# First norm of a hybrid decoder layer: two groups of tiles with a root each, all squares on ScalarE, the root's table loaded at the start

## The chip, the cores and the metric

The kernel runs on one core of one Trainium2 chip. The metric is the device time of one execution in microseconds (us). Engines: PE is TensorE (matmul), PEld its weight loads, DVE VectorE, ACT ScalarE, POOL GpSimd, SP SyncE, which here issues the DMAs.

## The reference

One layer on 16 learned meta tokens and 512 real tokens of width 2048. The change lies in the first `rms_norm`; everything else follows it.

```python
def rms_norm(x, g):
    xf = x.astype(jnp.float32)
    y = xf * lax.rsqrt(jnp.mean(xf * xf, axis=-1, keepdims=True) + RMS_EPS)
    return (y * g.astype(jnp.float32)).astype(x.dtype)

h = jnp.concatenate([meta, x], axis=1)
hn = rms_norm(h, ln_mix_g[l])
proj = hn @ w_in[l]                      # 2048 -> 5632 columns
...                                      # attention and HGRN2 on proj
h = h + jnp.concatenate([att, rec], axis=-1) @ w_out[l]
h = h[:, N_META:]
h = h + peer_ffn(rms_norm(h, ln_ffn_g[l]), ...)
```

## The kernel before, in words

The program is a row of blocks: first norm (tag `mixnorm`), projection, attention, recurrence, output product, second norm (tag `ffnnorm`), routing, gate tables, experts. In a block each engine has its own instruction list, the lists meet only through semaphores, and a barrier stands between blocks. Within an engine instructions start in the order written, so a wait holds all that is queued behind it.

`norm_rows` writes a norm block. The first norm has five sources in this order: the meta rows (16 partitions), then four tiles of 128 tokens (`x_rows`, tile numbers 0 to 3). SyncE issues, in order, two early constants, the meta rows, the four tiles (1 MB each), the first four pieces of `w_in` and the other constants; `loaded[i]` counts the landing of source i. `stat` holds small rows per tile: 0 the sum of squares, 1 the mean plus epsilon, 2 its square root, 3 the inverse root.

- ACT (L151 to L176) squares and sums the meta rows and tiles 0, 1 and 3 (L163), waiting for each landing and for its own previous sum; then takes one square root for all five sources (L167), splits the high parts of two pieces of `w_in` (L311), and copies 16 column blocks out of PSUM with the gain (`hn_high`, L172).
- DVE (L187 to L223) squares tile 2 (`by_dve`, L197), waits for all sums, makes the mean (L203), waits for the root, corrects it in five small chained operations (`inverse_root`, L102 to L106), scales the four tiles (L208) and the meta rows (L211), and then makes the low parts of the 16 column blocks (`hn_low`, L214) and of the meta rows (L219, L223).
- PE (L226 to L252) waits for each scaled tile and turns its first six column blocks with matmuls against the identity (L232, six PSUM banks), then the meta rows (L244), then the other ten column blocks, each as soon as DVE has emptied the bank of six blocks before.
- POOL narrows a mask that comes with the last constant (L2300) and subtracts the two low parts of `w_in` (L319).

The second norm uses the same function with `sums` given, hence without squares and with no meta rows.

Of the kernel before, what the change touches and what calls it, by code (L numbers as in the profile page):

```python
# [24 lines left out]
ALU = mybir.AluOpType  # L25
ACT = mybir.ActivationFunctionType
AX = mybir.AxisListType
F32 = mybir.dt.float32
# [4 lines left out]
P = 128  # L33
D = 2048
DC = D // P
T = 512
TB = T // P
# [8 lines left out]
EPS = 1e-6  # L46
# [13 lines left out]
class Count:  # L60
# [10 lines left out]
    def link(self, ins):  # L71

        self.up(ins)
        self.wait()
# [25 lines left out]
def inverse_root(dve, link, out, square, root, spare):  # L100

    link(dve.reciprocal(out, root))  # L102
    link(dve.tensor_tensor(spare, out, out, ALU.mult))
    link(dve.tensor_tensor(spare, spare, square, ALU.mult))
    link(dve.tensor_scalar(spare, spare, -0.5, 1.5, ALU.mult, ALU.add))
    link(dve.tensor_tensor(out, out, spare, ALU.mult))  # L106
# [5 lines left out]
def norm_rows(nc, tag, tiles, scaled_tiles, meta, gain, parts, columns, ident, place, kb, stream,  # L112
              loads, consts=None, sums=None, pool_first=None, pool_last=None, split_here=True):

    n = len(tiles) + (meta is not None)
    hi, lo = parts
    used = []
    with ExitStack() as ctx:
        def sem(name):
            used.append(ctx.enter_context(nc.semaphore(f"{tag}_{name}")))
            return used[-1]

        loaded = [sem(f"loaded{i}") for i in range(n)] if sums is None else []
        summed, summed_too, meaned, rooted = sem("summed"), sem("summed_too"), sem("meaned"), sem("rooted")  # L130
        scaled, turned, high, low = sem("scaled"), sem("turned"), sem("high"), sem("low")
        meta_turned, meta_whole_ready, meta_high = (sem("meta_turned"), sem("meta_whole_ready"),
                                                    sem("meta_high"))
        chain = sem("chain")
        stat = place(f"{tag}_stat", [P, 4, 8], F32, kb)
        squares = [place(f"{tag}_squares{i}", [P, D], F32, kb + 1 + 8 * i) for i in range(2)] \
            if sums is None else []
        meta_whole = place(f"{tag}_meta_whole", [P, DC, M], F32, kb + 17) if meta is not None else None
        banks = [ctx.enter_context(nc.psum_tensor(f"{tag}_bank{b}", [P, TB, P], F32)) for b in range(NORM_BANKS)]
        meta_bank = ctx.enter_context(nc.psum_tensor(f"{tag}_meta_bank", [P, DC, M], F32))  # L140
        block = ctx.enter_context(nc.Block())
        by_dve = 2

        def sources():

            return ([(meta, M, TB)] if meta is not None else []) + [(rows, P, tb) for tb, rows in enumerate(tiles)]

        @block.sync
        def _(sp):
            loads(sp, loaded)  # L150

        @block.scalar
        def _(act):
            act.wait_ge(chain, 1)
            if sums is None:
                count = 0
                for i, (rows, m, at) in enumerate(sources()):
                    if at == by_dve:
                        continue
                    act.wait_ge(loaded[i], 16)  # L160
                    if count:
                        act.wait_ge(summed, count)
                    act.activation(squares[0][0:m, :], rows, ACT.Square,  # L163
                                   accum_out=stat[0:m, 0, at:at + 1]).then_inc(summed, 1)
                    count += 1
            act.wait_ge(meaned, 1)
            act.activation(stat[:, 2, 0:n], stat[:, 1, 0:n], ACT.Sqrt).then_inc(rooted, 1)  # L167
            if split_here:
                stream.split_first_high(act)
            for c in range(DC):  # L170
                act.wait_ge(turned, c + 1)
                act.activation(columns(hi, c), banks[c % NORM_BANKS][:, :, :], ACT.Copy,  # L172
                               scale=gain[:, c:c + 1]).then_inc(high, 1)
            if meta is not None:
                act.wait_ge(meta_whole_ready, 1)
                act.copy(hi[:, :, 0:M], meta_whole[:, :, :]).then_inc(meta_high, 1)  # L176

        @block.gpsimd
        def _(pool):
            if pool_first:  # L180
                pool_first(pool)
            if split_here:
                stream.split_first_low(pool)
            if pool_last:
                pool_last(pool, scaled)

        @block.vector  # L187
        def _(dve):
            link = Count(dve, chain).link
            link(dve.memset(stat[:, 0, :], 1.0))  # L190
            if consts:
                dve.wait_ge(*consts)
            if sums is None:
                for i, (rows, m, at) in enumerate(sources()):
                    if at == by_dve:
                        dve.wait_ge(loaded[i], 16)
                        dve.scalar_tensor_tensor(squares[1][:, :], rows, 1.0, rows, ALU.mult, ALU.mult,  # L197
                                                 accum_out=stat[:, 0, at:at + 1]).then_inc(summed_too, 1)
                dve.wait_ge(summed, n - 1)
                dve.wait_ge(summed_too, 1)  # L200
            else:
                link(dve.tensor_reduce(stat[:, 0, 0:TB], sums[:, :, :], AX.X, ALU.add))
            dve.tensor_scalar(stat[:, 1, 0:n], stat[:, 0, 0:n], 1.0 / D, EPS,  # L203
                              ALU.mult, ALU.add).then_inc(meaned, 1)
            dve.wait_ge(rooted, 1)
            inverse_root(dve, link, stat[:, 3, 0:n], stat[:, 1, 0:n], stat[:, 2, 0:n], stat[:, 0, 0:n])
            for tb in range(TB):
                dve.tensor_scalar(scaled_tiles[tb], tiles[tb], stat[:, 3, tb:tb + 1], None, ALU.mult)\  # L208
                    .then_inc(scaled, 1)
            if meta is not None:  # L210
                dve.tensor_scalar(meta, meta, stat[0:M, 3, TB:TB + 1], None, ALU.mult).then_inc(scaled, 1)  # L211
            for c in range(DC):
                dve.wait_ge(high, c + 1)
                dve.scalar_tensor_tensor(columns(lo, c), banks[c % NORM_BANKS][:, :, :], gain[:, c:c + 1],  # L214
                                         columns(hi, c).bitcast(F32), ALU.mult, ALU.subtract)\
                    .then_inc(low, 1)
            if meta is not None:
                dve.wait_ge(meta_turned, 1)
                dve.tensor_tensor(meta_whole[:, :, :], meta_bank[:, :, :],  # L219
                                  gain[:, :].unsqueeze(2).to_broadcast([P, DC, M]), ALU.mult)\  # L220
                    .then_inc(meta_whole_ready, 1)
                dve.wait_ge(meta_high, 1)
                dve.tensor_tensor(hi[:, :, M:2 * M], meta_whole[:, :, :], hi[:, :, 0:M].bitcast(F32),  # L223
                                  ALU.subtract)

        @block.tensor  # L226
        def _(pe):
            if consts:
                pe.wait_ge(*consts)

            def turn(tb, c):
                return pe.transpose(banks[c % NORM_BANKS][:, tb, :], scaled_tiles[tb][:, c * P:(c + 1) * P],  # L232
                                    ident[:, :])

            for tb in range(TB):
                pe.wait_ge(scaled, tb + 1)
                for c in range(NORM_BANKS):
                    last = turn(tb, c)
                    if tb == TB - 1:
                        last.then_inc(turned, 1)  # L240
            if meta is not None:
                pe.wait_ge(scaled, n)
                for c in range(DC):
                    last = pe.transpose(meta_bank[:, c, :], meta[:, c * P:(c + 1) * P], ident[0:M, 0:M])  # L244
                last.then_inc(meta_turned, 1)
            for c in range(NORM_BANKS, DC):
                pe.wait_ge(low, c - NORM_BANKS + 1)
                for tb in range(TB):
                    last = turn(tb, c)
                last.then_inc(turned, 1)  # L250
    return used
# [2166 lines left out]
```

## Time and profile before

| | us |
|---|---|
| median of 3 runs | 3525.15 (3524.41 to 3530.05) |
| the profiled execution, its own time | 3515.08 |
| its span, first to last instruction | 3513.3 |
| PE busy | 3337.3 (95%) |
| DVE / ACT / POOL busy | 2222.2 / 1116.2 / 1186.5 |
| first norm, from the start to the first matmul of the projection | 38.08 |

A row of the timeline gives start, duration, engine, line, operation, out<-in, count, and in brackets how long the engine sat idle before it and what released it. A row with a count of several is merged; its duration then goes from the first start to the last end.

### The profile page before, as it was taken

The numbers are of one execution on the slowest core, as the hardware profiler recorded it, in microseconds if no ns is written. First come the engines' busy times: TensorE is split into PE (matmuls) and PEld (weight loads), VectorE is DVE, ScalarE is ACT, GpSimd is POOL, SyncE is SP. The second block draws the span as 40 slices with busy tenths as digits, with TensorE's granted clock in tenths as the row PEclk, the third lists the DMA queues.
The fourth block names the chain that finished last, engine by engine and source line by source line (L and its number), as shares of the span: only waits on it lengthen the run. The fifth ranks groups of instructions, "written<-read, shape, count | busy, mean of one in ns | idle before, by whom it ended". The sixth has DMA issues, their size and how long they took to land.

```text
span 3513.3 us, 51557 instructions
## 1 busy us (share of the span) xinstructions
PE 3337.3 (95%) x16860; PEld 2931.6 (83%) x16860; DVE 2222.2 (63%) x3869; ACT 1116.2 (32%) x1725; POOL 1186.5 (34%) x878
## 2 busy tenths in 40 slices
PE   7999999779989976799999999999999999999999
PEld 5778877667877866789989989989989989989998
DVE  2003413893038898677777777777777777777776
ACT  3222223443222279232232232332332322322322
POOL 2344441364435610323223233233233233333332
PEclk9999999999999999899999999999999999999999
DMA  4233320003322234878878788888878878878776
GB/s 142 78 90 96 96 84 16 25 1 118 99 101 85 84 126 203 291 261 277 262 261 278 258 263 278 259 261 273 266 261 274 264 260 271 268 259 275 265 260 235
DMA packets 294650, 686.94 MB, mean 196 GB/s; under 512 B 139040, under 2 KB 139296, under 8 KB 292000
## 3 DMA queue, kind: packets, MB, share of 16 engines
q1 hardware_dynamic: 220848, 417.52, 36.5%
q0 software_dynamic: 73728, 268.47, 22.7%
q8 instruction: 43, 0.70, 0.1%
q14 instruction: 31, 0.25, 0.0%
HBM read 655.48 MB, written 30.41 MB: 195 GB/s over the span
## 4 chain that ended last, share of the span: by engine, by line
PE 59%; ACT 2%; issue 1%; DMA 1%; DVE 1%; ACTq 0%; SPq 0%; POOL 0%; DVEq 0%; POOLq 0%
PE exp_a L2018 10%; PE exp_a L2020 10%; PE exp_a L2019 10%; PE exp_o L2039 10%; PE exp_o L2041 10%; PE exp_o L2037 10%; ACT table_gaps L1808 1%; ACT table_stage L1824 1%; DMA exp_rows<-in_u_rows,exp_now 0%; PE table_b L1768 0%; DMA gate_table<-table_stage 0%; DVE exp_rows L2123 0%; ACTq L1808 0%; DMA exp_act<-gate_table 0%; ACTq L1824 0%
## 5 line engine op out<-in xcount | busy, mean ns | idle before, releaser
L2020 PE MATMUL exp_a<-x_high,exp_ul 128*128 128x384 f32 x1984 | 663.1, 334 | 0.0
L2018 PE MATMUL exp_a<-x_high,exp_uh 128*128 128x384 f32 x1984 | 663.0, 334 | 0.0
L2019 PE MATMUL exp_a<-x_low,exp_uh 128*128 128x384 f32 x1984 | 662.9, 334 | 0.0
L2037 PE MATMUL exp_o<-exp_vh,exp_ah 128*128 128x512 f32 x1536 | 599.3, 390 | 27.4 <-DVE exp_al L2183 16.1
L2041 PE MATMUL exp_o<-exp_vh,exp_al 128*128 128x512 f32 x1536 | 599.4, 390 | 0.0
L2039 PE MATMUL exp_o<-exp_vl,exp_ah 128*128 128x512 f32 x1536 | 599.3, 390 | 0.0
L1999 POOL DMA_INDIRECT exp_rows<-in_v_rows,exp_now x256 | 330.4, 1290 | 706.9 <-DVE h L2130 655.4
L1999 POOL DMA_INDIRECT exp_rows<-in_u_rows,exp_now x256 | 299.9, 1171 | 704.4 <-DVE exp_rows L2123 658.9
L2069 ACT CAST exp_vh<-exp_raw 128x1024 fp32r<-128x1024 f32 x252 | 256.0, 1051 | 515.9 <-PE exp_o L2041 488.0
L2109 DVE TENSOR_TENSOR exp_vl<-exp_raw,exp_vh 128x1024 fp32r<-128x1024 f32 x256 | 304.4, 1220 | 155.0 <-ACT exp_vh L2069 146.0
L2018 PEld LDWEIGHTS exp_a<-x_high,exp_uh 128*128 128x128 f32 x1984 | 372.4, 188 | 1.2
L2019 PEld LDWEIGHTS exp_a<-x_low,exp_uh 128*128 128x128 f32 x1984 | 372.4, 188 | 1.2
L2020 PEld LDWEIGHTS exp_a<-x_high,exp_ul 128*128 128x128 f32 x1984 | 372.4, 188 | 0.0
L2080 ACT ACTIVATE exp_act<-exp_a 128x384 f32<-128x384 f32 x124 | 61.1, 492 | 950.0 <-PE exp_a L2020 807.6
L2037 PEld LDWEIGHTS exp_o<-exp_vh,exp_ah 128*128 128x128 f32 x1536 | 289.3, 188 | 87.3 <-issue 16.3
L2041 PEld LDWEIGHTS exp_o<-exp_vh,exp_al 128*128 128x128 f32 x1536 | 289.1, 188 | 60.2
L2039 PEld LDWEIGHTS exp_o<-exp_vl,exp_ah 128*128 128x128 f32 x1536 | 289.4, 188 | 59.5
L319 POOL TENSOR_TENSOR w_in_lo<-w_in_raw,w_in_hi 128x1024 fp32r<-128x1024 f32 x88 | 212.5, 2416 | 320.2 <-ACT w_in_hi L305 320.2
L2109 DVE TENSOR_TENSOR exp_ul<-exp_raw,exp_uh 128x1024 fp32r<-128x1024 f32 x248 | 300.2, 1221 | 31.1 <-ACT exp_uh L2069 31.1
L2130 DVE SCALAR_TENSOR_TENSOR h<-exp_rows,exp_weights,h 128x1024 f32<-128x1024 f32 x256 | 316.6, 1277 | 0.2 <-DMA exp_rows<-in_v_rows,exp_now 0.2
L2123 DVE SCALAR_TENSOR_TENSOR exp_rows<-exp_rows,sparse_x 128x1024 f32<-128x1024 f32 x256 | 302.7, 1217 | 10.6 <-DMA exp_rows<-in_u_rows,exp_now 10.5
L2150 DVE TENSOR_TENSOR exp_act<-exp_act,exp_gates 128x384 f32<-128x384 f32 x124 | 69.7, 562 | 356.7 <-ACT exp_act L2080 214.1
(302 smaller groups left out, 5263.3 us busy)
## 6 DMA issues: line engine op xcount, KB each, us to landing
exp_raw<-in_v SPq DMA_DIRECT2D x256, 512.0 KB
exp_raw<-in_u SPq DMA_DIRECT2D x248, 512.0 KB
w_in_raw<-in_w_in SPq DMA_DIRECT2D x88, 512.0 KB, 3.6
gate_table<-table_stage SPq DMA_DIRECT2D x5, 4096.0 KB, 11.5
exp_gates<-gate_table SPq DMA_DIRECT2D x126, 160.0 KB, 2.6
w_out_raw<-in_w_out SPq DMA_DIRECT2D x32, 512.0 KB, 3.7
w_q_raw<-in_w_q SPq DMA_DIRECT2D x32, 512.0 KB, 3.9
x_rows<-in_x SPq DMA_DIRECT2D x4, 1024.0 KB, 8.0
```

The lines of the kernel that those rows point to most:

```text
L319: eng.tensor_tensor(self.lo[:, g % 2], self.raw[:, g % RAW], self.hi[:, g % 2].bitcast(F32), ALU.subtract).then_inc(self.low, 1)
L1999: pool.indirect_dma_start(rows[slot][:, :], None, sparse["u" if kind == "dot" else "v"], bass.IndirectOffsetOnAxis(ap=now[:, turn, place_n ...
L2018: pe.matmul(bank, uh[:, b, c, :], xh[:, 0:DENSE_TB, c, :], start=(c == 0), stop=False)
L2019: pe.matmul(bank, uh[:, b, c, :], xl[:, 0:DENSE_TB, c, :], start=False, stop=False)
L2020: last = pe.matmul(bank, ul[:, b, c, :], xh[:, 0:DENSE_TB, c, :], start=False, stop=(c == DC - 1))
L2037: pe.matmul(bank[:, :], ah[:, key, tokens], vh[:, dc % 2, key, :], start=(key == 0), stop=False)
L2039: pe.matmul(bank[:, :], ah[:, key, tokens], vl[:, dc % 2, key, :], start=False, stop=False)
L2041: last = pe.matmul(bank[:, :], al[:, key, tokens], vh[:, dc % 2, key, :], start=False, stop=(key == KEYS_OF_MACRO - 1))
L2069: act.copy(part(uh if split[0] == "u" else vh, *split, half), raw[:, c % RAW_SLOTS, :])\
L2109: dve.tensor_tensor(part(ul if kind == "u" else vl, kind, which, half), raw[:, slot, :], part(uh if kind == "u" else vh, kind, which, half ...
L2123: done = dve.scalar_tensor_tensor(rows[slot][:, :], rows[slot][:, :], 1.0, sparse["x"][:, half, :], ALU.mult, ALU.mult, accum_out=dots[:, ...
L2130: done = dve.scalar_tensor_tensor(sums, rows[slot][:, :], weights[:, pl(pick(m, kind, t), 1)], sums, ALU.mult, ALU.add)
```

## The change

The first norm's five sources form two groups: tiles 0 and 1, and then tiles 2, 3 and the meta rows. Each group gets its own mean, root, inverse root and scaling. ACT takes all five sums of squares; the DVE square of tile 2 is gone. Before the first square ACT runs a square root over the eight freshly set ones of `stat` and writes a row that is overwritten later, so that the table that the root needs is the first one loaded. The root of the first group stands on ACT between the wait for tile 2's landing and tile 2's square. The second norm has one group, as before. The semaphore `summed_too` is replaced by `opened`, and one scratch tile of squares is gone.

```diff
-        by_dve = 2
+        groups = [slice(0, n)] if sums is not None else [slice(0, TB // 2), slice(TB // 2, n)]
...
         def _(act):
+            def root(g):
+                act.wait_ge(meaned, g + 1)
+                act.activation(stat[:, 2, groups[g]], stat[:, 1, groups[g]], ACT.Sqrt).then_inc(rooted, 1)
+
             act.wait_ge(chain, 1)
             if sums is None:
-                count = 0
+                act.activation(stat[:, 2, :], stat[:, 0, :], ACT.Sqrt).then_inc(opened, 1)
                 for i, (rows, m, at) in enumerate(sources()):
-                    if at == by_dve:
-                        continue
                     act.wait_ge(loaded[i], 16)
-                    if count:
-                        act.wait_ge(summed, count)
+                    if i == 0:
+                        act.wait_ge(opened, 1)
+                    else:
+                        act.wait_ge(summed, i)
+                    if at == groups[0].stop:
+                        root(0)
                     act.activation(squares[0][0:m, :], rows, ACT.Square,
                                    accum_out=stat[0:m, 0, at:at + 1]).then_inc(summed, 1)
-                    count += 1
-            act.wait_ge(meaned, 1)
-            act.activation(stat[:, 2, 0:n], stat[:, 1, 0:n], ACT.Sqrt).then_inc(rooted, 1)
+            root(len(groups) - 1)
...
             link(dve.memset(stat[:, 0, :], 1.0))
...
-            if sums is None:
-                for i, (rows, m, at) in enumerate(sources()):
-                    if at == by_dve:
-                        dve.wait_ge(loaded[i], 16)
-                        dve.scalar_tensor_tensor(squares[1][:, :], rows, 1.0, rows, ALU.mult, ALU.mult,
-                                                 accum_out=stat[:, 0, at:at + 1]).then_inc(summed_too, 1)
-                dve.wait_ge(summed, n - 1)
-                dve.wait_ge(summed_too, 1)
-            else:
+            if sums is not None:
                 link(dve.tensor_reduce(stat[:, 0, 0:TB], sums[:, :, :], AX.X, ALU.add))
-            dve.tensor_scalar(stat[:, 1, 0:n], stat[:, 0, 0:n], 1.0 / D, EPS,
-                              ALU.mult, ALU.add).then_inc(meaned, 1)
-            dve.wait_ge(rooted, 1)
-            inverse_root(dve, link, stat[:, 3, 0:n], stat[:, 1, 0:n], stat[:, 2, 0:n], stat[:, 0, 0:n])
-            for tb in range(TB):
-                dve.tensor_scalar(scaled_tiles[tb], tiles[tb], stat[:, 3, tb:tb + 1], None, ALU.mult)\
-                    .then_inc(scaled, 1)
+            for g, group in enumerate(groups):
+                if sums is None:
+                    dve.wait_ge(summed, n if group.stop == n else group.stop + 1)
+                dve.tensor_scalar(stat[:, 1, group], stat[:, 0, group], 1.0 / D, EPS,
+                                  ALU.mult, ALU.add).then_inc(meaned, 1)
+                dve.wait_ge(rooted, g + 1)
+                inverse_root(dve, link, *(stat[:, row, group] for row in (3, 1, 2, 0)))
+                for tb in range(group.start, min(group.stop, TB)):
+                    dve.tensor_scalar(scaled_tiles[tb], tiles[tb], stat[:, 3, tb:tb + 1], None, ALU.mult)\
+                        .then_inc(scaled, 1)
```

On ACT, from the start of the first norm to the split of `w_in`, the program before has these rows (`mixnorm_loaded0` is the landing of the meta rows, `loaded1` to `loaded4` those of tiles 0 to 3):

```order
-L163 ACT_TABLE_LOAD [waits mixnorm_loaded0]
-L163 ACTIVATE mixnorm_squares_115,mixnorm_stat<-meta_rows 16x2048 [waits mixnorm_chain]
-L163 ACTIVATE mixnorm_squares_115,mixnorm_stat<-x_rows 128x2048 [waits mixnorm_summed,mixnorm_loaded1]
-L163 ACTIVATE mixnorm_squares_115,mixnorm_stat<-x_rows 128x2048 [waits mixnorm_summed,mixnorm_loaded2]
-L163 ACTIVATE mixnorm_squares_115,mixnorm_stat<-x_rows 128x2048 [waits mixnorm_summed,mixnorm_loaded4]
-L167 ACT_TABLE_LOAD
-L167 ACTIVATE mixnorm_stat<-mixnorm_stat 128x5 [waits mixnorm_meaned]
-L311 CAST w_in_hi<-w_in_raw 128x1024 [waits w_in_loaded0]
```

In the changed program the same stretch of ACT reads:

```order
+L159 ACT_TABLE_LOAD
+L159 ACTIVATE mixnorm_stat<-mixnorm_stat 128x8 [waits mixnorm_chain]
+L168 ACTIVATE mixnorm_squares,mixnorm_stat<-meta_rows 16x2048 [waits mixnorm_opened,mixnorm_loaded0]
+L168 ACTIVATE mixnorm_squares,mixnorm_stat<-x_rows 128x2048 [waits mixnorm_summed,mixnorm_loaded1]
+L168 ACTIVATE mixnorm_squares,mixnorm_stat<-x_rows 128x2048 [waits mixnorm_summed,mixnorm_loaded2]
+L155 ACTIVATE mixnorm_stat<-mixnorm_stat 128x2 [waits mixnorm_meaned,mixnorm_summed,mixnorm_loaded3]
+L168 ACTIVATE mixnorm_squares,mixnorm_stat<-x_rows 128x2048
+L168 ACTIVATE mixnorm_squares,mixnorm_stat<-x_rows 128x2048 [waits mixnorm_summed,mixnorm_loaded4]
+L155 ACTIVATE mixnorm_stat<-mixnorm_stat 128x3 [waits mixnorm_meaned]
+L309 CAST w_in_hi<-w_in_raw 128x1024 [waits w_in_loaded0]
```

One table load is left, ahead of every landing; tile 2's square has come to ACT, and the first group's root stands ahead of it.

On DVE, the first norm before, up to the scaled meta rows:

```order
-L190 MEMSET mixnorm_stat 128x8
-L197 SCALAR_TENSOR_TENSOR mixnorm_squares_116,mixnorm_stat<-x_rows 128x2048
-L203 TENSOR_SCALAR mixnorm_stat<-mixnorm_stat 128x5
-L102 RECIPROCAL mixnorm_stat<-mixnorm_stat 128x5
-L103 TENSOR_TENSOR mixnorm_stat<-mixnorm_stat 128x5
-L104 TENSOR_TENSOR mixnorm_stat<-mixnorm_stat 128x5
-L105 TENSOR_SCALAR mixnorm_stat<-mixnorm_stat 128x5
-L106 TENSOR_TENSOR mixnorm_stat<-mixnorm_stat 128x5
-L208 TENSOR_SCALAR x_rows<-x_rows,mixnorm_stat 128x2048 x4
-L211 TENSOR_SCALAR meta_rows<-meta_rows,mixnorm_stat 16x2048
```

And in the changed program, from the end of the first group's inverse root on (the first group's mean and other chained operations, of 128x2, stand ahead of it in the same order as the second's):

```order
+L106 TENSOR_TENSOR mixnorm_stat<-mixnorm_stat 128x2
+L206 TENSOR_SCALAR x_rows<-x_rows,mixnorm_stat 128x2048 x2
+L201 TENSOR_SCALAR mixnorm_stat<-mixnorm_stat 128x3
+L102 RECIPROCAL mixnorm_stat<-mixnorm_stat 128x3
+L103 TENSOR_TENSOR mixnorm_stat<-mixnorm_stat 128x3
+L104 TENSOR_TENSOR mixnorm_stat<-mixnorm_stat 128x3
+L105 TENSOR_SCALAR mixnorm_stat<-mixnorm_stat 128x3
+L106 TENSOR_TENSOR mixnorm_stat<-mixnorm_stat 128x3
+L206 TENSOR_SCALAR x_rows<-x_rows,mixnorm_stat 128x2048 x2
+L209 TENSOR_SCALAR meta_rows<-meta_rows,mixnorm_stat 16x2048
```

Two of the four scalings now stand ahead of the last mean, and six small operations are added. The lists of PE, POOL and SP hold the same instructions in the same order as before.

## Rows read from the trace of the kernel before

**Rows 1.** The page: busy time and the span in 40 slices of 88 us.

```profile
PE 3337.3 (95%) x16860; PEld 2931.6 (83%) x16860; DVE 2222.2 (63%) x3869; ACT 1116.2 (32%) x1725; POOL 1186.5 (34%) x878
...
PE   7999999779989976799999999999999999999999
```

**Rows 2.** Busy time by stretch: start:end, length, each engine, granted clock, DMA share, GB/s.

```profile
37.00:43.00 6.00, 4.92 (x12) 3.89 (x13) 0.52 (x2) 0.01 (x1) 0.00 (x0) 0.50 0.47 128
44.00:50.00 6.00, 6.00 (x28) 4.59 (x27) 0.00 (x0) 1.05 (x1) 1.54 (x1) 1.00 0.00 1
50.00:550.00 500.00, 500.00 (x2162) 391.90 (x2160) 86.19 (x108) 116.61 (x134) 201.48 (x84) 1.00 0.30 86
550.00:1450.00 900.00, 756.80 (x4119) 641.24 (x4118) 597.97 (x1863) 386.89 (x819) 332.18 (x230) 0.94 0.28 97
1450.00:3513.30 2063.30, 2056.16 (x10463) 1878.98 (x10461) 1517.08 (x1866) 589.22 (x742) 645.51 (x557) 1.00 0.80 265
```

**Rows 3.** Timeline, ACT and DVE up to the root.

```profile
4.54 1.28 ACT L163 ACT_TABLE_LOAD   x1 [4.54 <-DMA meta_rows<-in_meta]
5.83 1.91 ACT L163 ACTIVATE mixnorm_squares<-meta_rows 16x2048 f32<-16x2048 f32 x1
7.92 1.91 ACT L163 ACTIVATE mixnorm_squares<-x_rows 128x2048 f32<-128x2048 f32 x1
10.02 1.91 ACT L163 ACTIVATE mixnorm_squares<-x_rows 128x2048 f32<-128x2048 f32 x1
12.19 2.29 DVE L197 SCALAR_TENSOR_TENSOR mixnorm_squares<-x_rows 128x2048 f32<-128x2048 f32 x1 [11.29 <-DMA x_rows<-in_x]
14.56 1.91 ACT L163 ACTIVATE mixnorm_squares<-x_rows 128x2048 f32<-128x2048 f32 x1 [2.54 <-DMA x_rows<-in_x]
16.38 0.19 ACT L163 ACTIVATION_READ_ACCUMULATOR mixnorm_squares<-x_rows 128x1 f32 x1
16.58 1.28 ACT L167 ACT_TABLE_LOAD   x1
16.60 0.17 DVE L203 TENSOR_SCALAR mixnorm_stat<-mixnorm_stat 128x5 f32<-128x5 f32 x1 [2.11 <-ACT mixnorm_squares L163]
17.88 0.21 ACT L167 ACTIVATE mixnorm_stat<-mixnorm_stat 128x5 f32<-128x5 f32 x1
17.99 1.98 ACT L311 CAST w_in_hi<-w_in_raw 128x1024 fp32r<-128x1024 f32 x2
```

**Rows 4.** Timeline, from the root to the last low part.

```profile
18.11 0.19 DVE L102 RECIPROCAL mixnorm_stat<-mixnorm_stat 128x5 f32<-128x5 f32 x1 [1.35 <-ACT mixnorm_stat L167]
19.14 4.88 DVE L208 TENSOR_SCALAR x_rows<-x_rows,mixnorm_stat 128x2048 f32<-128x2048 f32 x4
20.58 5.35 PE L232 MATMUL mixnorm_bank<-c_ident,x_rows 128*128 128x128 f32 x24 [20.58 <-DVE x_rows L208]
23.93 1.27 DVE L211 TENSOR_SCALAR meta_rows<-meta_rows,mixnorm_stat 16x2048 f32<-16x2048 f32 x1
24.90 9.37 ACT L172 ACTIVATE hn_high<-mixnorm_bank,c_ln_mix 128x512 fp32r<-128x512 f32 x16 [4.94 <-PE mixnorm_bank L232]
25.62 10.62 DVE L214 SCALAR_TENSOR_TENSOR hn_low<-mixnorm_bank,c_ln_mix,hn_high 128x512 fp32r<-128x512 f32 x16 [0.42 <-ACT hn_high L172]
```

**Rows 5.** Timeline, the weight loads of the turning matmuls.

```profile
20.55 4.98 PEld L232 LDWEIGHTS mixnorm_bank<-c_ident,x_rows 128*128 128x128 f32 x24 [20.55 <-issue]
27.16 1.73 PEld L232 LDWEIGHTS mixnorm_bank<-c_ident,x_rows 128*128 128x128 f32 x16
29.06 0.42 PEld L232 LDWEIGHTS mixnorm_bank<-c_ident,x_rows 128*128 128x128 f32 x4 [0.17 <-DVE hn_low L214]
```

**Rows 6.** Timeline, POOL in the first norm and the block's end.

```profile
26.82 0.93 POOL L2300 CAST c_level_mask<-level_mask_wide 128x896 uint8<-128x896 f32 x1 [26.35 <-DMA level_mask_wide<-in_level_mask]
27.80 4.70 POOL L319 TENSOR_TENSOR w_in_lo<-w_in_raw,w_in_hi 128x1024 fp32r<-128x1024 f32 x2
37.05 0.42 DVE L223 TENSOR_TENSOR hn_high<-mixnorm_meta_whole,hn_high 128x256 fp32r<-128x256 f32 x1 [0.47 <-ACT hn_high L176]
38.08 0.76 PE L364 MATMUL proj_bank<-w_in_hi,hn_high 128*128 128x512 f32 x1 [5.06 <-DVEq L517]
```

**Rows 7.** Timeline, matmuls of the projection: two starts early, two later.

```profile
39.06 0.63 PE L366 MATMUL proj_bank<-w_in_lo,hn_high 128*128 128x512 f32 x1
39.49 0.63 PE L364 MATMUL proj_bank<-w_in_hi,hn_high 128*128 128x512 f32 x1
...
44.10 0.39 PE L365 MATMUL proj_bank<-w_in_hi,hn_low 128*128 128x512 f32 x1
44.33 0.40 PE L366 MATMUL proj_bank<-w_in_lo,hn_high 128*128 128x512 f32 x1
```

More of the change, by code:

```diff
@@ L129, in norm_rows @@
         loaded = [sem(f"loaded{i}") for i in range(n)] if sums is None else []
-        summed, summed_too, meaned, rooted = sem("summed"), sem("summed_too"), sem("meaned"), sem("rooted")
+        summed, opened, meaned, rooted = sem("summed"), sem("opened"), sem("meaned"), sem("rooted")
         scaled, turned, high, low = sem("scaled"), sem("turned"), sem("high"), sem("low")
@@ L135, in norm_rows @@
         stat = place(f"{tag}_stat", [P, 4, 8], F32, kb)
-        squares = [place(f"{tag}_squares{i}", [P, D], F32, kb + 1 + 8 * i) for i in range(2)] \
-            if sums is None else []
+        squares = [place(f"{tag}_squares", [P, D], F32, kb + 1)] if sums is None else []
         meta_whole = place(f"{tag}_meta_whole", [P, DC, M], F32, kb + 17) if meta is not None else None
```

## The prediction

> **What bounds the kernel now.** I read the page first. PE is busy for 95% of the span, and only a few of its forty slices fall below nine tenths [rows 1]. The table of stretches says where: from 50 to 550 us PE is busy for all of the 500 us, and from 1450 us to the end for 2056 of 2063 us; between, it is busy for 757 of 900 us [rows 2]. So behind the first norm PE is nearly always at work. The weight loads from memory follow PE's pace there, because each buffer is refilled only when its use is over. A time by which the projection starts earlier should therefore reach the end of the span unchanged. The first norm itself is the one part that the change touches: PE's first matmul of the projection starts at 38.08 us [rows 6].
>
> Next I read the timeline of those 38 us and followed the wait that ends last. Tile 3 lands at 14.56 us, when ACT starts its square [rows 3]; tile 2 landed at 12.19 us, when DVE started. ACT's sum is out at 16.57 us (16.38 + 0.19). DVE makes the mean (16.60 + 0.17 = 16.77), but the root starts only at 17.88, since ACT loads a table from 16.58 for 1.28 us [rows 3]. DVE's chain runs from 18.11, the four scalings start at 19.14, the meta rows' at 23.93 [rows 4]. The last tile is scaled shortly before, PE turns it, ACT makes its first high part at 24.90 and DVE the first low part at 25.62. From there DVE goes through 16 low parts in 10.62 us, 0.66 each, and bounds the rest; its last operation ends at 37.47, and PE starts 0.61 later [rows 4, 6]. Thus the path is: landing of tile 3, square, mean, table and root, chain, four scalings, turn, 16 low parts, meta rows.
>
> **The change, part by part.**
>
> *The table load.* Before, two loads; after, one, ahead of all landings, as the order shows. The first one ran from 4.54 to 5.82 while tiles were still on their way [rows 3]. Having it earlier gains nothing, because the square of tile 3 still waits for 14.56. The second lay on the path. Now the root can start when the mean is out, 16.77 plus the 0.03 us that a hand-over takes (17.88 + 0.21 = 18.09 against 18.11, and 16.57 against 16.60) [rows 3, 4], thus at 16.80 in place of 17.88: **gain 1.08**. The dummy root at the start costs some 0.21 us [rows 3] between 1 and 4.5 us, where ACT waits for the meta rows: 0 on the path. The load's cover is the 4.54 us before the meta rows land; without it, it would cost at most its 1.28 at the start, and even then ACT would be back on the landings by tile 3.
>
> On the price of a load, the row shows 1.28 us, and 1.30 us from its start at 16.58 to the root's start at 17.88 [rows 3]. The Trainium skill (ScalarE: Activation LUTs, section "What ACT_TABLE_LOAD costs") states about 1.28 us for the load and about 1.38 us more for a drain, some 2.66 us for each switch. This trace agrees with the load and shows no drain beside it. By the page's price, as an estimate, the gain of this part would be some 2.4 in place of 1.08.
>
> *The square of tile 2.* On DVE it took 2.29 us plus its read-out; ACT's start one after another every 2.10 us (7.92, 10.02) [rows 3]. ACT now has root, square 2 and square 3 behind the landing at 12.19. The root takes 0.11 us of the queue (17.88 to 17.99, where the next instruction starts) [rows 3]. Square 2 starts at 12.30, square 3 could start at 14.40, and tile 3 lands at 14.56. **Cost 0**, with 0.16 us of cover. Were tile 2 to land later or tile 3 earlier, each tenth beyond that would be lost; if they landed together the loss would be some 2.2. I take 0, with 0.3 as the upper end, from landings that differ by a few tenths. The mean of the first group needs the sums of the meta rows, tile 0 and tile 1. ACT will start the meta rows at about 4.54 and not 5.83, so tile 1's square starts no later than 10.02, its sum is out by 12.02 and the mean by 12.22: the wait ahead of the first root ends with tile 2's landing, or 0.03 later. What is queued behind that wait is square 2 alone.
>
> The same page (section "Rules for kernel authors") says that multiplications belong on VectorE, not on ScalarE. The trace does not bear this out for this f32 square: 2.10 us from start to start on ACT against 2.29 on DVE. What hangs on it is only whether square 3 is late, and by the rows it is not.
>
> *The first group.* Its root ends about 12.5. DVE's chain from the reciprocal to the first scaling takes 1.03 us (18.11 to 19.14), and scalings start every 1.20 us ((23.93 − 19.14)/4) [rows 4]. So tiles 0 and 1 are scaled from about 13.5 to 16.0. DVE must be free for the second mean at 16.60; 0.6 us of cover. The scalings run beside DMA traffic and beside ACT, as they did before. So the six added small operations cost 0, and **two scalings leave the path: gain 2 × 1.20 = 2.40**. If the cover failed, DVE would be late by what is over, at most a few tenths.
>
> *The second group.* Mean at 16.60, root 16.80 to 17.01, chain from 17.03, tile 2 scaled from 18.06, tile 3 from 19.26, meta rows from 20.46. Before it was 23.93: 3.47 sooner. The high part of `w_in` (1.98 us on ACT) starts at 16.9 and ends at 18.9, long before ACT's first high part at about 21.4. It needs its two pieces on the chip; they were there at 17.99, and if the first came at just that time ACT would still end near 20.
>
> *Turning.* Twenty-four weight loads took 4.98 us, 0.21 each, at first; sixteen took 1.73, 0.108 each, from 27.16 on [rows 5]. PE thus ran at half pace at first, and had little slack against DVE's 1.20 us per tile (24 matmuls in 5.35). Now it turns tiles 0 and 1 early and comes to tile 3 without a backlog: between 0 and 0.2 gained, I take 0. If PE stayed at the slow pace through the whole of the norm, four matmuls would take 0.86 us against DVE's 0.66. Six full banks stand ahead; over ten blocks PE falls 2.0 us behind and has about 1.0 of lead, so 1.0 is the upper end of the cost. I take 0, since PE is at work without a long pause from 19.4 on, longer than before.
>
> *The end of the block.* POOL is fixed by a landing at 26.35, which the change doesn't move, and ends at 32.50 (27.80 + 4.70) [rows 6]. DVE now ends at 34.00. **POOL is late next**, with 1.5 us of cover. It limits any gain to about 5.0.
>
> The sum: 1.08 + 2.40 = 3.48, with bounds of 2.2 (0.3 and 1.0 lost) to 3.7 (0.2 won). Against the profiled execution this is a span of 3513.3 − 3.5 = 3509.8 and a time of 3515.08 − 3.5 = 3511.6. That execution lies 10 us below the median of the runs shown, and 9.3 below the lowest of them. Against the median: **3525.15 − 3.5 = 3521.6**, or 0.10% faster. A change within 0.2% (7 us) is about what a measurement of this kernel can't tell from none.
>
> **The rivals.**
>
> *(a) As summed*, 3521.6: 0.60.
>
> *(b) PE's clock doesn't fall ahead of the projection.* The granted clock was 0.50 from 37 to 43 us and 1.00 from 44 on [rows 2], after PE had sat idle for 5.06 us [rows 6]; these are the levels of 1.2 and 2.4 GHz. Matmuls started every 0.43 us and later every 0.23 [rows 7]. From 38.08 to about 43.5 that is 12.7 matmuls of 0.20 more, 2.5 us. The change leaves the idle stretch as long as it was, so it should fall again; but it may not, or may last for another length. If not: 3519.1. Chance 0.12.
>
> *(c) A table switch costs more than its row shows.* In this kernel ACT would have stood still beyond the 1.28 us before; the rows leave 0.02 us for that (17.88 − 16.58 − 1.28). A further 1.4 us would give 3520.2. The page named above has this rule. Chance 0.03.
>
> *(d) The gain does not arrive.* The barrier behind the norm waits for POOL. If the mask landed at 30.9 and not at 26.35, POOL would end at 37.0 and nothing would be won: 3525. Against it: the same DMAs are issued in the same order, and their landing waited for nothing on ACT or DVE. Chance 0.05.
>
> *(e) The clock in the middle, the slower side.* Between 550 and 1450 us the mean granted clock is 0.94 [rows 2]: some 108 us at the lower level (0.06 × 2 × 900), worth up to 54 us. Where PE pauses there, and when the clock follows, may change when everything starts 3.5 us sooner. Break-even is 7 us more at the lower level; 20 us more would cost 10 and give 3531.6. For it: executions of the same program differ by 5.6 us here, and by 15 with the profiled one. Against it: it isn't bound to the change and has no sign. Slower side 0.07, and the faster side, down to some 3512, 0.13, for the profiled execution shows that such times occur.
>
> **How the numbers follow.** The time is that of (a). The range takes in (a) to (d), 3519 to 3525, and the nearer part of both sides of (e): 3513.5 to 3528.5, leaving out less than 0.2. Faster by over 0.2% needs 7 us: most of the fast side of (e) and a tail of (a) and (b), 0.14. Slower by over 0.2%: most of the slow side of (e), 0.05. The rest, 0.81, is within 0.2%.
>
> **What would show it.** In the changed kernel's profile: one table load before 4.5 us, none near 16.6; square of tile 2 at 12.3 and of tile 3 at 14.56, still released by the DMA; two scalings between 13.5 and 16.0; root at 16.8; meta rows scaled from 20.5; first low part at 22.1; DVE's end at 34.0 and the projection's first matmul at 34.6. Wrong would be: tile 3's square released by ACT's own sum, the second mean released by DVE's own scaling, a POOL row released at the barrier, or a projection start at 34.6 with a span that isn't 3.5 shorter; then the difference lies in the granted clock between 550 and 1450 us.

## The result, and the profile after

The changed kernel takes 3533.43 us (median of 20 runs, 3522.13 to 3545.20); the kernel before, beside it, 3523.87 us (20 runs, 3511.97 to 3537.23). The ratio is 1.0030 with a 95% interval of 1.0019 to 1.0042: it is **slower by some 10 us** (7 to 15 by the interval), where 3.5 us less was forecast, and 3533.43 lies above the forecast range of 3513.5 to 3528.5. The profiled execution took 3527.13 us, with a span of 3525.3, against 3515.08 and 3513.3 before.

The norm itself did nearly what was forecast. Timeline of the changed kernel, the rows that answer to [rows 3, 4, 6]:

```profile
0.75 1.28 ACT L159 ACT_TABLE_LOAD   x1 [0.75 <-PEq L2409]
12.42 1.89 ACT L168 ACTIVATE mixnorm_squares<-x_rows 128x2048 f32<-128x2048 f32 x1
13.53 2.48 DVE L206 TENSOR_SCALAR x_rows<-x_rows,mixnorm_stat 128x2048 f32<-128x2048 f32 x2
14.83 1.91 ACT L168 ACTIVATE mixnorm_squares<-x_rows 128x2048 f32<-128x2048 f32 x1 [0.42 <-DMA x_rows<-in_x]
17.07 0.21 ACT L155 ACTIVATE mixnorm_stat<-mixnorm_stat 128x3 f32<-128x3 f32 x1 [0.23 <-DVE mixnorm_stat L201]
20.72 1.27 DVE L209 TENSOR_SCALAR meta_rows<-meta_rows,mixnorm_stat 16x2048 f32<-16x2048 f32 x1
22.17 11.39 DVE L212 SCALAR_TENSOR_TENSOR hn_low<-mixnorm_bank,c_ln_mix,hn_high 128x512 fp32r<-128x512 f32 x16 [0.18 <-ACT hn_high L175]
27.09 0.69 ACT L175 ACTIVATE hn_high<-mixnorm_bank,c_ln_mix 128x512 fp32r<-128x512 f32 x1 [0.17 <-PE mixnorm_bank L230]
35.39 0.47 PE L362 MATMUL proj_bank<-w_in_hi,hn_high 128*128 128x512 f32 x1 [4.26 <-DVEq L515]
```

The one table load stands at the start, two scalings run from 13.53 on, the root follows the mean at once, and the meta rows are scaled 3.21 us sooner (23.93 − 20.72). The projection starts at 35.39, 2.69 sooner. The forecast gain was 3.48. Of the missing 0.79 us, 0.27 is the landing of tile 3 (14.83 against 14.56), and 0.77 the 16 low parts, which took 11.39 and not 10.62: the high part at 27.09 waits for PE, one of five such waits, since PE was turning at the slower pace there (these high parts lie 0.85 us apart, four matmuls of 0.21). Against this, 0.24 was won between the meta rows' scaling and the first low part (1.45 us in place of 1.69).

The loss lies far behind, in the routing, which the change does not touch. Busy time by stretch, each from the first PE instruction of attention, routing, gate tables and experts to the next stage's (columns as in [rows 2]); the kernel before:

```profile
572.80:660.90 88.10, 71.00 (x427) 55.79 (x427) 62.58 (x138) 50.49 (x127) 3.40 (x6) 0.95 0.04 13
1013.60:1257.70 244.10, 229.13 (x1089) 194.38 (x1089) 185.72 (x902) 61.86 (x77) 129.11 (x54) 0.98 0.25 78
1257.70:1460.40 202.70, 140.74 (x924) 124.10 (x925) 177.08 (x502) 149.16 (x354) 25.75 (x23) 0.90 0.57 221
1460.40:3513.30 2052.90, 2045.76 (x10417) 1870.35 (x10415) 1506.67 (x1851) 586.41 (x739) 639.94 (x554) 1.00 0.80 265
```

and the changed kernel:

```profile
569.20:663.40 94.20, 78.95 (x426) 61.87 (x426) 62.79 (x138) 50.46 (x127) 3.38 (x6) 0.84 0.04 12
1016.00:1268.90 252.90, 228.41 (x1089) 193.90 (x1089) 198.00 (x902) 61.86 (x77) 129.13 (x54) 0.97 0.25 75
1268.90:1472.50 203.60, 141.92 (x925) 124.47 (x926) 177.93 (x503) 149.12 (x354) 27.05 (x23) 0.90 0.57 222
1472.50:3525.30 2052.80, 2045.70 (x10417) 1870.30 (x10415) 1505.87 (x1850) 586.56 (x739) 639.89 (x553) 1.00 0.80 265
```

Read the third busy column, DVE, in the second row of each: the same 902 instructions are busy for 198.00 us in place of 185.72, and the stretch is 8.8 us longer. The experts take the same to 0.1 us. Attention is 6.1 us longer, at a granted clock of 0.84 against 0.95; that part turned out to belong to the execution, not to the kernel (below). The two profiled spans differ by 12.0 us, and the stages add up to it: 2.7 and 0.9 less up to attention, 6.1 more in attention, 0.1 less up to the routing, 8.8 more in the routing, 0.9 more in the gate tables and 0.1 less in the experts.

Where on DVE? The same four operations, one behind the other, in the routing, kernel before:

```profile
1115.17 0.23 DVE L1676 SCALAR_TENSOR_TENSOR route_pos_f<-route_quarterf 128x64 f32<-128x64 f32 x1
1115.43 0.23 DVE L1678 SCALAR_TENSOR_TENSOR route_pos_f<-route_pos_f,route_quarterf 128x64 f32<-128x64 f32 x1
1115.69 0.23 DVE L1680 TENSOR_TENSOR route_pos_f<-route_pos_f,route_quarterf 128x64 f32<-128x64 f32 x1
1116.06 2.35 DVE L1643 TENSOR_REDUCE picks<-route_hot 128x1024 f32 x2
```

changed kernel (its lines are two lower):

```profile
1114.89 0.22 DVE L1674 SCALAR_TENSOR_TENSOR route_pos_f<-route_quarterf 128x64 f32<-128x64 f32 x1
1115.15 2.43 DVE L1676 SCALAR_TENSOR_TENSOR route_pos_f<-route_pos_f,route_quarterf 128x64 f32<-128x64 f32 x1
1117.61 0.23 DVE L1678 TENSOR_TENSOR route_pos_f<-route_pos_f,route_quarterf 128x64 f32<-128x64 f32 x1
1117.98 2.35 DVE L1641 TENSOR_REDUCE picks<-route_hot 128x1024 f32 x2
```

An operation of 0.23 us stands there with 2.43: the next one came 2.2 us late, and no wait is given for it. More such places follow in later passes, at L1667, L1678 and L1683. Grouped by line over the routing, the changed kernel shows the eight calls of L1676 with a mean of 500 ns and those of L1678 with 757:

```profile
L1678 DVE TENSOR_TENSOR route_pos_f<-route_pos_f,route_quarterf 128x64 f32<-128x64 f32 x8 | 6.1, 757 | 0.3
L1676 DVE SCALAR_TENSOR_TENSOR route_pos_f<-route_pos_f,route_quarterf 128x64 f32<-128x64 f32 x8 | 4.0, 500 | 0.3
```

where the kernel before has 225 for both:

```profile
L1678 DVE SCALAR_TENSOR_TENSOR route_pos_f<-route_pos_f,route_quarterf 128x64 f32<-128x64 f32 x8 | 1.8, 225 | 0.3
L1680 DVE TENSOR_TENSOR route_pos_f<-route_pos_f,route_quarterf 128x64 f32<-128x64 f32 x8 | 1.8, 225 | 0.3
```

The kernel before isn't free of such places. Two of them:

```profile
1063.81 2.41 DVE L1675 CAST route_quarterf<-route_pos 128x256 f32<-128x256 uint32 x1
1230.90 2.33 DVE L1654 CAST route_idx_f<-route_idx 128x128 f32<-128x128 uint32 x1 [0.24 <-DVE route_idx L1631]
```

I call a stall here a DVE row that lasts over 0.4 us longer than the median row of the same operation, shape and tiles. The routing of the kernel before then has 5 stalls, with 8.9 us in all; that of the changed kernel has 12, with 21.6 us, and these 12.7 us more are about what DVE's busy time has more (12.3). The second half of the routing is a loop of three passes of 288 DVE instructions. The kernel before stalls twice ahead of the loop, twice in its last pass and once behind it; the changed kernel stalls in every pass.

How it reaches PE is in the changed kernel's timeline, POOL and PE:

```profile
1177.18 4.75 POOL L1478 TENSOR_TENSOR route_hot<-route_hot,route_idx_f 128x1024 f32<-128x1024 f32 x2 [5.04 <-DVE route_hot L1683]
1181.88 4.71 POOL L317 TENSOR_TENSOR w_q_lo<-w_q_raw,w_q_hi 128x1024 fp32r<-128x1024 f32 x2
...
1184.29 0.50 PE L362 MATMUL route_q<-x_high,w_q_hi 128*128 128x512 f32 x1 [3.51 <-POOL w_q_lo L317]
```

POOL waits for DVE's late `route_hot`, the low part of the weights is queued behind it, and PE waits for that. Ahead of the same `route_hot` POOL sat idle for 2.70 us before and 5.04 now. Over the whole routing PE idles 15.0 us before (244.1 − 229.13) and 24.5 now (252.9 − 228.41): of DVE's 12.3 us more, 9.5 arrive at PE.

### The profile page after: what moved, and what is told of

It reads as the page before. It is cut to its first block, busy times and chain, and to the rows that moved or that the text cites. A ratio compares the mean times of both kernels' runs of the same rounds, so it can differ in the third digit from the quotient of the medians.

```text
span 3525.3 us, 51564 instructions
## 1 busy us (share of the span) xinstructions
PE 3346.7 (95%) x16860; PEld 2939.8 (83%) x16860; DVE 2233.9 (63%) x3873; ACT 1117.9 (32%) x1728; POOL 1188.5 (34%) x878
## 4 chain that ended last, share of the span: by engine, by line
PE 59%; ACT 2%; issue 1%; DMA 1%; DVE 0%; ACTq 0%; SPq 0%; POOL 0%; DVEq 0%; POOLq 0%
PE exp_a L2018 10%; PE exp_a L2016 10%; PE exp_a L2017 10%; PE exp_o L2037 10%; PE exp_o L2035 10%; PE exp_o L2039 10%; ACT table_gaps L1806 2%; ACT table_stage L1822 1%; DMA exp_rows<-in_u_rows,exp_now 0%; DMA gate_table<-table_stage 0%; PE table_b L1766 0%; DVE exp_rows L2121 0%; ACTq L1806 0%; ACTq L1822 0%; SPq L1950 0%
```

## The experiments

Two theories. **P, place:** the change lengthens DVE's instruction list by three (six small operations more; the square, its read-out and one separate wait less), so everything later on DVE, the routing too, lies at other places in the list and stalls at other instructions. **S, shift:** the earlier start itself moves the pauses of PE against the chip's decisions on its clock, and the loss is the clock's. All ratios are against the kernel before on the same chip.

**b_dve3** puts three one-element memsets into the kernel before, while DVE idles:

```diff
             link(dve.memset(stat[:, 0, :], 1.0))
+            if sums is None:
+                for k in range(3):
+                    dve.memset(pads[:, k:k + 1], 0.0)
```

> The kernel before with three one-element memsets added on VectorE, before its wait for the first tile, where it idles until 12.2 us: its instruction list is then as long as the changed kernel's, its timing in the norm is unchanged. Theory P (place in the instruction list: what comes later on VectorE is fetched at other places, and stalls there): slower than the kernel before by 5 to 13 us. Rival S (the earlier start itself, through PE's clock): same as before, within 3 us.

Measured: 3540.83 us against 3526.55, ratio 1.0039 (1.0019 to 1.0059). The memsets end by 1.1 us of an idle time that lasts to 12.18, and the projection starts at 38.1 as before. The routing's stretch, where the same 902 instructions show 201.98 us:

```profile
1026.40:1284.80 258.40, 233.99 (x1089) 197.93 (x1089) 201.98 (x902) 61.86 (x77) 128.97 (x54) 0.94 0.24 74
```

Three instructions that cost nothing where they stand make the kernel 14 us slower by the medians (7 to 21 by the interval). S falls as the main cause: nothing started earlier.

**b_act4** lengthens ScalarE's list instead, **b_dve3_act4** both:

```diff
             act.wait_ge(chain, 1)
             if sums is None:
+                for k in range(5):
+                    act.activation(pads[:, 256 + k:257 + k], stat[:, 0, 5 + k % 3:6 + k % 3], ACT.Square)
```

> The kernel before with five one-element squares added on ScalarE while it waits for the meta rows; one separate wait is merged into them, so its list is longer by four, as the changed kernel's. Theory P with ScalarE as the engine: slower by 5 to 13 us. Theory P with VectorE as the engine, and rival S: within 3 us of the kernel before.

> The kernel before with both paddings, so that both lists are as long as in the changed kernel, and nothing starts earlier. Theory P: slower by about 13 us, which is what the changed kernel lost (10) plus what its norm gained (3). Rival S: same as before, within 3 us.

Measured: b_act4 3523.57 us, ratio 0.9999 (0.9978 to 1.0019); b_dve3_act4 3538.44 us, 1.0036 (1.0017 to 1.0056). Their routings, in this order:

```profile
1020.00:1264.00 244.00, 229.01 (x1088) 194.19 (x1089) 185.73 (x902) 61.83 (x77) 129.10 (x54) 0.98 0.25 78
```

```profile
1013.70:1269.00 255.30, 230.90 (x1088) 195.63 (x1089) 200.47 (x902) 61.83 (x77) 128.97 (x54) 0.95 0.24 75
```

So it is DVE's list, and ScalarE's longer list does nothing here that the interval (0.9978 to 1.0019) can show. b_act4 places the same scratch tile for its padding as b_dve3, so the tile isn't the cause either. The traces bear out the counts: with the rows of semaphores and registers, which no view counts as busy, DVE has 6895 rows in the kernel before and in b_act4, and 6898 in the changed one; ACT has 3334 before and 3338 in the other two.

**a_late** takes the changed kernel's gain away without touching the length of a list:

```diff
+        for g in range(3):
+            w_in.load(sp, 0, g, ahead=True)
         for tb in range(TB):
             sp.dma_start(x_rows[:, tb, :], ...)
...
-        w_in.load_start(sp)
+        w_in.load(sp, 0, 3, ahead=True)
```

> The changed kernel with three of the four first pieces of w_in loaded ahead of the tiles of x in place of behind them: all lists keep their lengths, and the tiles land some 3.7 us later, which takes the norm's gain back. Theory P: slower than the changed kernel by a further 3 to 4 us, thus about 13 over the kernel before. Rival S: the loss goes with the earlier start, so back to the kernel before within 3 us.

Measured: 3539.61 us, ratio 1.0034 (1.0014 to 1.0054); the projection starts at 38.9. Its routing takes 257.6 us, with DVE busy for 201.53 in it. The loss stays when the early start is gone. That is against S; the difference to the changed kernel (0.0004 in the ratio) is too small to tell the expected 3 to 4 us from none.

**a_short** keeps the two groups and takes the three instructions out again, by a shorter inverse root in both norms:

```diff
+            def short_root(out, square, root, spare):
+                link(dve.reciprocal(out, root))
+                link(dve.tensor_tensor(spare, out, out, ALU.mult))
+                link(dve.tensor_tensor(spare, spare, square, ALU.mult))
+                link(dve.scalar_tensor_tensor(out, spare, 3.0, out, ALU.subtract, ALU.mult))
...
-                inverse_root(dve, link, *(stat[:, row, group] for row in (3, 1, 2, 0)))
+                short_root(*(stat[:, row, group] for row in (3, 1, 2, 0)))
...
-                    dve.tensor_scalar(scaled_tiles[tb], tiles[tb], stat[:, 3, tb:tb + 1], None, ALU.mult)\
+                    dve.tensor_scalar(scaled_tiles[tb], tiles[tb], stat[:, 3, tb:tb + 1], -0.5, ALU.mult, ALU.mult)\
```

> The changed kernel with the inverse root in four chained operations in place of five (the factor -0.5 goes into the scaling), in both norms: VectorE's list is then as long as that of the kernel before, the norm keeps its two groups. Theory P (place in VectorE's list): the norm's gain stays and the loss goes, so 3 to 4 us faster than the kernel before and 13 faster than the changed one; in the trace the head loop of the routing takes 49.8 and 52.5 us for its two later passes as before, not 52.4 and 58.6. Rival (something else of the change, which the paddings only hit by chance): slower than before by some 10.

Measured: 3518.65 us against 3525.49, ratio 0.9982 (0.9970 to 0.9994): faster than the kernel before, and by the ratios than the changed one. The projection starts at 34.3, the two later passes of the loop take 49.8 and 52.5 us as forecast (52.4 and 58.6 in the changed kernel), and the routing:

```profile
1008.80:1249.90 241.10, 226.11 (x1088) 192.21 (x1089) 184.14 (x902) 61.84 (x77) 129.16 (x54) 0.99 0.26 79
```

Its 16 low parts in the norm again take 10.62 us:

```profile
21.77 10.62 DVE L218 SCALAR_TENSOR_TENSOR hn_low<-mixnorm_bank,c_ln_mix,hn_high 128x512 fp32r<-128x512 f32 x16 [0.19 <-ACT hn_high L175]
```

**a_dve125, a_dve253 and b_dve64** are the same memsets in other numbers, the first two in the changed kernel, the last in the kernel before.

> The changed kernel with 125 one-element memsets on VectorE ahead of its first wait, some 4 us of its idle 11: the list's later part is moved by 128 in all against the kernel before. Theory P with a grid of 128 instructions (8 KB at 64 bytes each, the size of one kind of instruction packets in the trace): as the kernel before less the norm's gain, 3 to 4 us faster than before. Theory P with a longer grid: slower than before, or another time altogether. Rival (no grid): slower than before by 10.

> The changed kernel with 253 such memsets, some 8 us of the idle 11: moved by 256 in all against the kernel before. Theory P with a grid of 128 or of 256 instructions: 3 to 4 us faster than before. If this one is faster and the one with 125 is not, the grid is 256 (16 KB, the other size of instruction packets).

> The kernel before with 64 such memsets. Theory P: another place, so another time, anywhere from 10 us faster to 20 slower, with VectorE's stalls in the routing at other instructions than before and than with three. Rival (only the number of instructions counts, each one costing a little): 21 times the cost of three memsets, which can't be.

Measured: 3519.78 us, ratio 0.9991 (0.9977 to 1.0006); 3522.28, 0.9997 (0.9981 to 1.0012); 3537.06, 1.0034 (1.0020 to 1.0049). Their routings, in this order:

```profile
1017.10:1261.00 243.90, 228.88 (x1089) 194.24 (x1090) 185.86 (x902) 61.86 (x77) 129.20 (x54) 0.98 0.25 78
```

```profile
1024.30:1268.50 244.20, 229.21 (x1089) 194.44 (x1090) 185.83 (x902) 61.84 (x77) 129.12 (x54) 0.98 0.25 78
```

```profile
1014.40:1272.50 258.10, 233.18 (x1088) 197.22 (x1089) 201.53 (x902) 61.87 (x77) 129.33 (x54) 0.95 0.24 74
```

Adding 125 or 253 instructions to the changed kernel removes its loss; adding 64 to the kernel before makes one. It isn't the number that counts but where the routing comes to lie, and moves of 128 and 256 in all act as a move of 0. That fits a grid of 128 instructions but does not show one, since other moves turn out harmless too (below). A grid of 64 is excluded by b_dve64. The two padded kernels show only part of the forecast 3 to 4 us: their projection starts at 35.0 and 36.0, thus 3.1 and 2.1 us sooner than before, and neither ratio is clear of 1.

One half of theory P failed: the stalls do not come to stand at other instructions. The first one of the routing is at the same conversion in the kernel before (above, 1063.81), with 64 instructions more, and with 32 more in s_dve32 (below):

```profile
1064.50 2.36 DVE L1679 CAST route_quarterf<-route_pos 128x256 f32<-128x256 uint32 x1
```

```profile
1069.88 2.41 DVE L1683 CAST route_quarterf<-route_pos 128x256 f32<-128x256 uint32 x1
```

The same holds inside the loop: in the six kernels with the long routing the stalls stand at the same instructions, or at most three instructions away, whether the move is 1, 3 or 64. So the place decides whether the passes of the loop stall, not at which instructions.

**s_dve1, s_dve32, s_dve96, s_dve120** put such memsets into a_short, to see which moves are bad.

> The changed kernel with the shorter inverse root (a_short) and one memset on VectorE at the start, so that its list lies one instruction off the kernel before in place of three. If the edge of the stalls lies at the first instruction, the routing takes 253 to 258 us; if later, 241 to 244 as without it. No theory says which; the time follows the routing.

> The same with 32 memsets. Theory P: the stalls stand at other instructions of the routing; its length lies anywhere between 235 and 260 us, and the whole time moves by what the routing moves, with the spread of the attention stage's clock on top.

> The same with 96 memsets; expectation as for 32. The loop's body of 288 instructions is 32 longer than two steps of 128, so there should be places where each pass crosses one step less, and there the routing is shortest.

> The same with 120 memsets, eight instructions short of a full step of 128. If the stalls begin for moves of 1 or 3 forward and not for moves backward, this one keeps the routing at 241 to 244 us and the time within 0.2% of a_short.

Measured: 3529.74 us, ratio 1.0013 (0.9998 to 1.0029); 3521.58, 0.9991 (0.9976 to 1.0005); 3519.19, 0.9995 (0.9979 to 1.0010); 3519.29, 0.9981 (0.9966 to 0.9997). The routing of s_dve1, one memset more than a_short:

```profile
1009.00:1264.20 255.20, 231.01 (x1088) 195.78 (x1089) 201.07 (x902) 61.88 (x77) 129.07 (x54) 0.95 0.24 75
```

One instruction is enough for 14.1 us of routing (255.2 against 241.1) and for 8 to 11 us of the median (3529.74 against 3519.19 to 3521.58 in the other three, on the same chip). The others' routings take 241.2, 244.1 and 241.4 us. Two expectations missed: in s_dve32 the stalls stand where they stood, and s_dve96 is not the shortest. That of s_dve120 came true. All profiled executions, by the move of the routing in DVE's list against the kernel before:

| move | kernels | routing, us | DVE busy in it, us |
|---|---|---|---|
| 0, 128, 256 | before, b_act4, a_short, a_dve125, a_dve253 | 241.1 to 244.2 | 184.1 to 185.9 |
| 1 | s_dve1 | 255.2 | 201.1 |
| 3 | changed, b_dve3, b_dve3_act4, a_late | 252.9 to 258.4 | 198.0 to 202.0 |
| 32 | s_dve32 | 241.2 | 184.6 |
| 64 | b_dve64 | 258.1 | 201.5 |
| 96, 120 | s_dve96, s_dve120 | 244.1, 241.4 | 186.2, 185.0 |

Among the nine moves tried there are two kinds of places and nothing between. By the count above, the eight kernels with the short routing have 5 stalls each, with 7.5 to 8.9 us, and the six with the long one 12 or 13, with 21.6 to 25.1 us. None of the places tried is much better than that of the kernel before.

## Why the prediction was wrong

- **The step that failed** is the first: "A time by which the projection starts earlier should therefore reach the end of the span unchanged", and with it "So the six added small operations cost 0". They do cost nothing where they stand; but they move all that follows on DVE in its list, and in the routing DVE then stalls in every pass of the loop, by some 2.2 us each at the clearest ones. The mean routing is 256.2 us in the six kernels of the long kind and 243.0 in the eight of the short kind: a term of +13.2 that the sum lacked. With the forecast gain of 3.5 it gives +9.7; the medians differ by 9.6. That closeness is luck: the one pair of profiles shows +8.8 for the routing and a gain of 2.69 at the projection, and the interval of the ratio leaves 7 to 15 us.
- **The table's term** (1.08) was right in mechanism: the root starts 0.03 us after the mean's end (16.87 + 0.17 to 17.07), as forecast. The Trainium skill's further 1.38 us for a drain (ScalarE: Activation LUTs, "What ACT_TABLE_LOAD costs") doesn't show after either: the first load starts at 0.75 and the dummy root at 2.05, 1.30 us later. (By the page's price the gain would be 1.08 + 1.38 = 2.46 us; the prediction has 2.4.)
- **The two scalings' term** (2.40) was right too: with the table's and the landing's 0.27 it gives the 3.21 us by which the meta rows are scaled sooner.
- **The cover of tile 3's square** held: it was released by the landing, after 0.42 us of idle time. Tiles 0 and 1 were done at 16.01, 0.86 us ahead of the second mean.
- **"Between 0 and 0.2 gained, I take 0"**, for the turning, came out at 0.24.
- **"If PE stayed at the slow pace"** was taken as 0 with an upper end of 1.0. It came out as 0.77 in this execution, and 0 in a_short's; the term is the execution's.
- **Rival (b)** occurred in part. The clock did fall, but at 35.84, 0.45 us behind the projection's start, and it rose at 39.25:

```profile
35.00:35.50 0.50, 0.11 (x1) 0.14 (x2) 0.09 (x1) 0.00 (x0) 0.00 (x0) 1.00 0.00 0
35.50:36.00 0.50, 0.50 (x3) 0.35 (x4) 0.00 (x0) 0.00 (x0) 0.00 (x0) 0.84 0.00 0
```

Before, it fell at 36.64, ahead of the projection, and the projection ran at the lower level from 38.08 to 43.47. So 3.4 us at 1.2 GHz stand against 5.4, which gave back some 0.9 us (projection to attention 533.8 us against 534.7). PE's idle time ahead of the projection wasn't the same either: 4.26 us against 5.06.

- **Rival (d)** did not occur: POOL ended at 32.41 (27.73 + 4.68), ahead of DVE's 34.78.
- **Rival (e)** named the clock of the middle rightly as a source of spread, but not the cause of the result. Attention takes 87.9 to 100.4 us in the fourteen profiled executions, with a granted clock of 0.97 where it took 88.0 (a_short) and 0.75 where it took 100.4 (b_dve3):

```profile
568.70:656.70 88.00, 69.42 (x427) 54.77 (x427) 62.63 (x138) 50.49 (x127) 3.42 (x6) 0.97 0.04 13
572.40:672.80 100.40, 86.79 (x426) 67.70 (x426) 62.85 (x138) 50.46 (x127) 3.38 (x6) 0.75 0.03 11
```

It does so in kernels of either kind: 100.4 in b_dve3 and 88.2 in b_dve3_act4, which share DVE's list. Without attention and routing the fourteen spans lie at 3176.2 to 3181.0 us, but for a_late with 3186.8, so these two stages make nearly all the differences between the profiles. Whether attention also makes the 25 us by which executions of one kernel differ isn't shown: no kernel was profiled twice, and 12.5 us is what attention shows. The prediction's last sentence, that a span not 3.5 shorter would lie in the granted clock between 550 and 1450 us, holds for the 6.1 us of attention in the one pair of profiles, not for the loss in the medians. The forecast "within 0.2%" with 0.81 treated everything outside the norm as noise around an unchanged kernel.

Left open: what the stall is. The Trainium skill (Vector Engine (DVE) Microarchitecture Reference, "Instruction fetch and dispatch (NX sequencer)") states that an instruction is 64 bytes wide; the page of the profile lists instruction packets of two sizes, 31 of one kind with 0.25 MB, thus 8 KB each, which would be 128 instructions. That a list's next piece is fetched late is thus a natural reading, but it is only argued. No packet was tied to a stall, and their number does not go with the stalls: within the routing there are 7 packets of the larger and 5 of the smaller kind in the kernel before, with 5 stalls, as in the changed kernel with 12 and in b_dve3 with 13, while b_dve64, with 13, has 7 and 16. Nor is it clear why moves of 1, 3 and 64 are bad and those of 32, 96 and 120 are not.

## What to carry to other kernels

In this kernel an edit that added one instruction on DVE brought stalls into a loop that it didn't touch. Whether other code is as sensitive isn't shown. Where a result lies far from the forecast, compare by stage the busy time of the same number of instructions, and run the kernel before with as many idle instructions as the edit adds: that tells the edit's own effect from that of its place. And before a small gain is given up, try it with the list's length restored; here that turned 10 us lost into 7 us won by the medians (2 to 11 by the interval).

## What the runs showed of the hardware

- Three one-element memsets, done in 0.1 us of idle time, made a kernel of 3.5 ms slower by 0.39% (0.19 to 0.59). Moves of 32, 96, 120, 128 and 256 instructions acted as none; moves of 1, 3 and 64 lengthened one stage from 241 to 244 us to 253 to 258.
- The profile shows such a stall not as idle time but as the length of the instruction ahead of it (2.43 us for one of 0.23), so it hides in the busy column. A count beside the busy time gives it away.
- Executions of one kernel spread over 25 us. Attention's length in the fourteen profiles (87.9 to 100.4 us) went with the clock that was granted there (0.97 to 0.75).
